# A hybrid encoder block on one core: how the first token block and the warming products start

## The reference

```python
h = rms_norm(x, mix_norm_g[l])
proj = h @ w_in[l]
u_a, v_a, q, k, v = jnp.split(proj, splits, axis=-1)
y_a = spatial_gating(u_a, v_a, sgu_ln_g[l], sgu_ln_b[l], sgu_w[l], sgu_b[l])
y_b = window_sink_attention(...)
x = x + jnp.concatenate([rms(y_a), rms(y_b)], axis=-1) @ w_out[l]
h = rms_norm(x, ffn_norm_g[l])
x = x + (jax.nn.silu(h @ w_gate[l]) * (h @ w_up[l])) @ w_down[l]
return rms_norm(x, final_norm_g)
```

## Time and profile before

| | |
|---|---|
| median of 3 runs | 918.92 us (918.57 to 918.98) |
| the profiled execution | 919.09 us, of which the span of the engines' instructions is 917.3 us |
| PE busy | 909.7 us, 99% of the span |
| PEld, DVE, ACT, POOL busy | 82%, 64%, 47%, 43% |
| chain of work that ended last | PE 98%, issue 1%, all others 0% |
| DMA over the span | 158.56 MB, 173 GB/s |

### The profile page before, as it was taken

How to read it: one execution, slowest core, us unless ns; L and a number is a source line. 1 busy time by engine, 2 the same in 40 slices (tenths; PEclk the granted TensorE clock), 3 DMA queues, 4 the chain that set the end, 5 groups by cost and what they waited for, 6 DMA issues and landing times.

```text
span 917.3 us, 11969 instructions
## 1 busy us (share of the span) xinstructions
PE 909.7 (99%) x4229; PEld 750.0 (82%) x4229; DVE 588.9 (64%) x785; ACT 429.6 (47%) x835; POOL 390.4 (43%) x387
## 2 busy tenths in 40 slices
PE   9999999999999999999999999999999999999997
PEld 7888888787878888888888888888888888888885
DVE  5759879986779787464453653736547676544754
ACT  6747547856556543243333333333334454444451
POOL 1559732331244379557485574855754000000021
PEclk9999999999999999999999999999999999999999
DMA  9797453211242372744727437264366996656543
GB/s 330 235 267 232 115 161 105 80 70 70 92 138 88 97 220 69 232 136 134 228 68 233 138 126 227 76 226 146 121 223 248 372 368 192 201 187 203 185 138 138
DMA packets 151487, 158.56 MB, mean 173 GB/s; under 512 B 27576, under 2 KB 109060, under 8 KB 151428
## 3 DMA queue, kind: packets, MB, share of 16 engines
q1 hardware_dynamic: 150756, 157.40, 53.0%
q10 hardware_dynamic: 672, 0.40, 0.1%
HBM read 117.26 MB, written 40.50 MB: 172 GB/s over the span
## 4 chain that ended last, share of the span: by engine, by line
PE 98%; issue 1%; ACT 0%; POOL 0%; DVE 0%; POOLq 0%; ACTq 0%
PE ps L859 31%; PE ps L861 31%; PE ps L860 31%; PE ps L1031 1%; PE ps L1054 1%; PE ps L1043 1%; PE ps L979 1%; PE ps L1125 1%; PE ps L883 0%; PE ps L892 0%; PE ps L895 0%; PE ps L898 0%; PE ps L1000 0%; PE ps L990 0%; PE ps L1061 0%
## 5 line engine op out<-in xcount | busy, mean ns | idle before, releaser
L2116 DVE TENSOR_TENSOR P_lo<-P_raw,P_hi 128x512 fp32r<-128x512 f32 x132 | 119.5, 921 | 83.2 <-ACT P_hi L1554 78.8
L859 PE MATMUL ps<-T_hi,P_hi 128*128 128x512 f32 x352 | 136.9, 389 | 0.0
L860 PE MATMUL ps<-T_lo,P_hi 128*128 128x512 f32 x352 | 136.9, 389 | 0.0
L861 PE MATMUL ps<-T_hi,P_lo 128*128 128x512 f32 x352 | 136.9, 389 | 0.0
L801 POOL TENSOR_TENSOR wd<-wd 128x256 f32<-128x256 f32 x88 | 80.9, 919 | 93.6 <-DMA wd<-in_w_down 88.4
L859 PE MATMUL ps<-rb_hi,ra_hi 128*128 128x512 f32 x308 | 119.8, 389 | 0.0
L860 PE MATMUL ps<-rb_lo,ra_hi 128*128 128x512 f32 x308 | 119.8, 389 | 0.0
L861 PE MATMUL ps<-rb_hi,ra_lo 128*128 128x512 f32 x308 | 119.8, 389 | 0.0
L1668 ACT ACTIVATE ra_hi<-ra 128x512 fp32r<-128x512 f32 x77 | 48.6, 631 | 98.8 <-DMA rb<-w_down_T 61.0
L649 POOL TENSOR_SCALAR late<-late 128x1 f32<-128x1 f32 x12 | 6.0, 503 | 191.7 <-ACT junk L1736 178.1
L2225 DVE TENSOR_TENSOR ra_lo<-ra,ra_hi 128x512 fp32r<-128x512 f32 x77 | 55.7, 723 | 36.4 <-ACT ra_hi L1668 36.0
(11 more groups left out here) (286 smaller groups left out, 2018.0 us busy)
## 6 DMA issues: line engine op xcount, KB each, us to landing
wd<-in_w_down SPq DMA_DIRECT2D x44, 256.0 KB, 3.3
w_down_T<-wd SPq DMA_DIRECT2D x22, 512.0 KB, 5.0
ra<-act_S SPq DMA_DIRECT2D x44, 256.0 KB, 2.7
rb<-w_down_T SPq DMA_DIRECT2D x44, 256.0 KB, 3.0
act_S<-Q SPq DMA_DIRECT2D x33, 256.0 KB, 3.7
ra<-act_A SPq DMA_DIRECT2D x33, 256.0 KB, 4.4
rb<-in_w_down SPq DMA_DIRECT2D x33, 256.0 KB, 5.0
P_raw<-in_w_gate SPq DMA_DIRECT2D x22, 256.0 KB, 3.7
```

Source lines behind the costliest of these rows:

```text
L859: mm(dst, lhs[0], rhs[0], start=start, stop=False, skip_group_check=onto)
L860: mm(dst, lhs[0], rhs[1], start=False, stop=False, skip_group_check=onto)
L861: return mm(dst, lhs[1], rhs[0], start=False, stop=stop, skip_group_check=onto)
L2116: tt(w_l[p, m][:], src[:], w_h[p, m][:].bitcast(F32), ALU.subtract).then_inc(w_split, 1)
```

## The change

GpSimd first fills a new 128x128 tile `zeros` (in the space of `v_sb0`, which is first written long after), and then does what it did. The warming products now take `zeros` as both operands, in `fp32r` and as plain products, not as transposes; there are 18 of them; and they wait for the first fill alone. TensorE's wait for `ident` stands behind them.

The tokens of block 0 come in two loads of 256 columns: the first counts into a new semaphore `hT0_in`, to which the gains' load moves too; the second into `block_in[0]`. VectorE rounds each half by itself, and TensorE starts with the first half's two tiles. ScalarE's first rounding waits for the weights alone. VectorE also rounds the tokens of block 1 (`hT_hi[0]`, k = 1), which was ScalarE's work. The counts of the waits on `hT_hi_ready` go down by one for that.

```diff
--- before.py
+++ after.py
@@ -67,6 +67,7 @@
     wv_hi, wv_lo = at("wv_hi", 64, [P, K, C], F32R), at("wv_lo", 80, [P, K, C], F32R)
     xs = [at(f"xs{s}", 96 + 4 * s, [P, D]) for s in range(4)]
     v_sb = [at(f"v_sb{s}", 112 + 2 * s, [P, DA]) for s in range(4)]
+    zeros = at("zeros", 112, [P, P], F32R)
     by_offset = at("by_offset", 120, [CH, HB, KW])
     rel_rep = at("rel_rep", 126, [CH, NBUCK, HB])
     w_hi = [at(f"w_hi{s}", 128 + 8 * s, [P, K, P], F32R) for s in range(2)]
@@ -294,7 +295,7 @@
         return IN_PRODUCTS + NP * i + IDX[p, m] + 1
 
 
-    WARM = 15
+    WARM = 18
 
     ROOT_BANK, MIX_BANK = (2, 7), (3, 4)
 
@@ -306,7 +307,8 @@
         def sem(name):
             return ctx.enter_context(nc.semaphore(name))
 
-        ident_set, ident_ready, consts_ready, zero_ready = (sem(n) for n in ("ident_set", "ident_ready", "consts_ready", "zero_ready"))
+        fill_set, ident_ready, consts_ready, zero_ready = (sem(n) for n in ("fill_set", "ident_ready", "consts_ready", "zero_ready"))
+        hT0_in = sem("hT0_in")
         wv0_in, rel_in, setup_in, ffng_in, fin_in = (
             sem(n) for n in ("wv0_in", "rel_in", "setup_in", "ffng_in", "fin_in"))
         bias_out, bias_in, rel_built = sem("bias_out"), sem("bias_in"), sem("rel_built")
@@ -369,9 +371,15 @@
                 sp.dma_start(xs[r % 4][:], xt[r]).then_inc(x_in[r % 4], 16)
 
             def xT_load(h, k):
-                if h:
-                    sp.wait_ge(hT_hi_ready, max(k, 1))
-                sp.dma_start(hT_raw[h][:, k, :], xT[h, k]).then_inc(block_in[k], 16)
+                if h and k < 2:
+                    sp.wait_ge(hT0_hi_ready, k + 2)
+                elif h:
+                    sp.wait_ge(hT_hi_ready, k - 1)
+                if h or k:
+                    sp.dma_start(hT_raw[h][:, k, :], xT[h, k]).then_inc(block_in[k], 16)
+                else:
+                    sp.dma_start(hT_raw[0][:, 0, 0:2 * P], xT[0, 0, :, 0:2 * P]).then_inc(hT0_in, 16)
+                    sp.dma_start(hT_raw[0][:, 0, 2 * P:C], xT[0, 0, :, 2 * P:C]).then_inc(block_in[0], 16)
 
             def item_load(n):
                 sp.dma_start(raw[n][:].rearrange("p (k n) -> p k n", k=K), w_in_k[:, :, COL[ITEMS[n]]:COL[ITEMS[n]] + P]).then_inc(raw_in[n], 16)
@@ -639,9 +647,10 @@
 
         @block.gpsimd
         def _(pool):
-            nc.gpsimd.memset(ident[:], 0.0).then_inc(ident_set, 1)
+            nc.gpsimd.memset(zeros[:].bitcast(F32), 0.0).then_inc(fill_set, 1)
+            nc.gpsimd.memset(ident[:], 0.0).then_inc(fill_set, 1)
             nc.gpsimd.memset(minus_half, -0.5).then_inc(consts_ready, 1)
-            pool.wait_ge(ident_set, 1)
+            pool.wait_ge(fill_set, 2)
             nc.gpsimd.affine_select(out=ident[:], in_=ident[:], compare_op=ALU.not_equal, fill=1.0, base=0,
                                     pattern=[[-1, P]], channel_multiplier=1).then_inc(ident_ready, 1)
 
@@ -878,17 +887,17 @@
                     last = nc.tensor.transpose(ps[:, ROOT_BANK[h], t * P:(t + 1) * P], rstd_x[:, r:r + 1].to_broadcast([P, P]), ident[:])
                 last.then_inc(rstd_T, 1)
 
+            pe.wait_ge(fill_set, 1)
+            for n in range(WARM):
+                mm(ps[:, 0, 0:P], zeros[:], zeros[:], start=True, stop=True)
             pe.wait_ge(ident_ready, 1)
-            for n in range(WARM):
-                nc.tensor.transpose(ps[:, 0, 0:P], ident[:], ident[:])
 
             for k in range(2):
-                if k:
-                    pe.wait_ge(hT_hi_ready, k)
-                else:
-                    pe.wait_ge(hT0_hi_ready, 1)
+                pe.wait_ge(hT0_hi_ready, 3 if k else 1)
                 pe.wait_ge(wv_hi_ready, k + 1)
                 for t in range(HT):
+                    if k == 0 and t == 2:
+                        pe.wait_ge(hT0_hi_ready, 2)
                     mm(ps[:, t, :], hT_hi[0][:, k, t * P:(t + 1) * P], wv_hi[:, k], start=k == 0, stop=False)
                 pe.wait_ge(wv_split, k + 1)
                 for t in range(HT):
@@ -1250,7 +1259,7 @@
 
             def wv_block(k):
                 if k == 0:
-                    act_e.wait_ge(wv0_in, 32)
+                    act_e.wait_ge(wv0_in, 16)
                 else:
                     act_e.wait_ge(block_in[k], LOADED[k])
                 actv(wv_hi[:, k, :], wv_raw[k // 2][:, k % 2, :], ACT.Copy).then_inc(wv_hi_ready, 1)
@@ -1267,10 +1276,12 @@
                 act_e.wait_ge(raw_in[n], 16)
                 actv(w_hi[n][:].rearrange("p k n -> p (k n)"), raw[n][:], ACT.Copy).then_inc(w_hi_ready, 1)
 
-            act_e.dma_start(mix_g, mix_gT).then_inc(wv0_in, 16)
+            act_e.dma_start(mix_g, mix_gT).then_inc(hT0_in, 16)
             for k in range(K):
                 wv_block(k)
-                if k:
+                if k == 1:
+                    act_e.wait_ge(hT0_in, 32)
+                if k > 1:
                     xT_block(0, k)
             for r in range(HT):
                 xT_block(1, 2 * r)
@@ -1761,10 +1772,10 @@
             copy = nc.vector.tensor_copy
 
             def xT_lo(h, k):
-                if h or k:
-                    dve.wait_ge(hT_hi_ready, K * h + k)
-                else:
-                    dve.wait_ge(hT0_hi_ready, 1)
+                if h or k > 1:
+                    dve.wait_ge(hT_hi_ready, K * h + k - 1)
+                else:
+                    dve.wait_ge(hT0_hi_ready, k + 2)
                 stt(hT_lo[h][:, k, :], hT_raw[h][:, k, :], mix_g[:, k:k + 1], hT_hi[h][:, k, :].bitcast(F32), ALU.mult, ALU.subtract).then_inc(hT_ready, 1)
 
             def wv_block(k):
@@ -1819,10 +1830,14 @@
                                   sinks_rep[rows].rearrange("p (g a b) -> p g a b", g=KV, a=2)[:, :, :, t2], -1.0, None, ALU.mult)
                 last.then_inc(sinks_ready, 1)
 
-            dve.wait_ge(wv0_in, 32)
+            dve.wait_ge(hT0_in, 32)
+            ts(hT_hi[0][:, 0, 0:2 * P], hT_raw[0][:, 0, 0:2 * P], mix_g[:, 0:1], None, ALU.mult).then_inc(hT0_hi_ready, 1)
             dve.wait_ge(block_in[0], LOADED[0])
-            ts(hT_hi[0][:, 0, :], hT_raw[0][:, 0, :], mix_g[:, 0:1], None, ALU.mult).then_inc(hT0_hi_ready, 1)
+            ts(hT_hi[0][:, 0, 2 * P:C], hT_raw[0][:, 0, 2 * P:C], mix_g[:, 0:1], None, ALU.mult).then_inc(hT0_hi_ready, 1)
             for k in range(K):
+                if k == 1:
+                    dve.wait_ge(block_in[1], LOADED[1])
+                    ts(hT_hi[0][:, 1, :], hT_raw[0][:, 1, :], mix_g[:, 1:2], None, ALU.mult).then_inc(hT0_hi_ready, 1)
                 wv_block(k)
                 xT_lo(0, k)
             xT_lo(1, 0)
```

## The result

| | before | with the change |
|---|---|---|
| median | 918.58 us (22 runs, 917.68 to 919.15) | 919.94 us (22 runs, 918.59 to 923.09) |
| ratio | | 1.0015, 95% interval 1.0009 to 1.0021 |
| profiled execution | 919.09 us, span 917.3 | 919.11 us, span 917.3 |
| PE busy | 909.7 us | 910.2 us |

The change makes the kernel 1.4 us slower. That is within the 0.2% that was called "same", but the interval excludes no change, and 919.94 lies above the forecast range of 917.1 to 919.0. The two profiled executions differ by 0.02 us (919.09 and 919.11): the one lies near the upper end of the runs of its kernel, the other near the lower end. So a comparison of these two traces shows how each step goes, but not what it costs in the median; the medians of the experiments have to tell that.

A forecast was written before the change was run, and what follows sets the result against it. TensorE, busy 909.7 of 917.3 us, was taken as the bound. Block 2 starting at 10.17 + 0.1 = 10.3 instead of 11.82 took 919.09 to 917.6; the median, 0.17 lower, gave 917.4 us, range 917.1 to 919.0.

The forecast's parts named there:

- TensorE sets the end, and what the start loses goes through: Whole kernel: TensorE sets the end from 1.5 us on, so what its first products gain reaches the end.
- Zeros first; start at 0.97: Start of warming: GpSimd fills zeros from 0.72 to 0.92, so TensorE starts at 0.97, not 1.51.
- 0.213 for each product: Warming on TensorE: each 128x128 zero product takes 0.213 us at the low clock, 18 of them 3.83.
- The clock is up by the first real product: TensorE's start: clock rises at about 4.0, first real product at 4.6, block 2 starts 1.5 us sooner.
- 0.1 + 5.47: From TensorE's first real product to block 2: 0.1 us filling plus 5.47 for 24 products at the high clock.
- The transposes had not raised the clock: Warming before the change: 3.4 us of transposes left the clock low; it rose 2.5 us into real products.
- nearly all there is to win: First eight real products: the low clock costs 3.20 - 1.82 = 1.38 us, nearly the whole possible gain.
- first rival: TensorE's warming: clock rises as before, at about 7.4; time 918.7 to 918.9; chance 0.22.
- second rival: TensorE's clock: rise shifts from run to run, gain anywhere from 0 to 1.5 us, middle 918.1; chance 0.10.
- The data for the first product: Block 0's load: first half of tokens lands at 4.05, rounding costs 0.27, ready at about 4.4.
- One more DMA issue, 0 to 0.25 us: SyncE's loads: the extra issue takes 0.47 us, mostly hidden; block 1 delays TensorE by 0 to 0.25, taken as 0.1.
- VectorE rounds block 1: Block 1's tokens: rounded by 7.03, needed at 7.44; without this part TensorE would have waited 0.4 us.

The follow-up runs named there:

- e6_zeros512: Kernel before with 9 warming products of 512 columns on zeros in place of the 15 transposes: 918.15 us, ratio 0.9998.
- e9_rows: Kernel before with block 0's tokens loaded by two DMAs of 64 rows each: 918.86 us against 918.47, ratio 1.0007.
- e1_warm: Kernel before with 18 products of 128x128 on zeros in place of the 15 transposes, nothing else changed: 919.94 us against 918.48, ratio 1.0013.
- e11_nowarm: Kernel before with its 15 warming transposes taken out, nothing else changed: 920.12 us against 918.63, ratio 1.0014.
- e5_ones128: Kernel before with 18 products of 128x128 on a tile of ones in place of the 15 transposes: 919.31 us, ratio 1.0012.
- e7_ones512: Kernel before with 9 warming products of 512 columns on ones in place of the 15 transposes: 918.24 us, ratio 1.0000.
- e8_best: Kernel before with 8 zero products of 512 columns reading a 128-column tile four times over, VectorE rounding block 1, one token load: 918.17 us against 918.47, ratio 0.9998.
- e3_dve1: Kernel before with VectorE instead of ScalarE rounding block 1's tokens, nothing else changed: 918.61 us, ratio 1.0001.
- e2_split: Kernel before with block 0's tokens in two loads of 256 columns, nothing else changed: 918.91 us against 918.48, ratio 1.0008.
- e10_after512: The whole change with 9 warming products of 512 columns on zeros in place of 18 of 128: 918.84 us against the kernel before, ratio 1.0003.

## Why the prediction was wrong

*TensorE sets the end, and what the start loses goes through.* Right: no later wait took it up or gave it back. In all fourteen traces the time of the profiled execution is the start of block 2 plus 906.9 to 907.4 us, though that start lies anywhere from 10.69 (e6_zeros512, 917.86 us) to 13.06 (e9_rows, 920.03).

*Zeros first; start at 0.97.* Right, 0.98. *0.213 for each product.* Right to the digit.

*The clock is up by the first real product.* This step failed, and with it the sign. The forecast took its price from the right rows and then let the clock rise at about 4.0 with nothing but the kind of the instruction to rest on. With the short zero products the first eight real ones still ran mostly at the low clock, and the median was that without warming (e1_warm 919.94, e11_nowarm 920.12). Ones in the tile made no difference that shows (e5_ones128 919.31). Where the clock was up by the first real product, as in the trace of e6_zeros512, the price was right: block 2 came 10.69 - 4.98 = 5.71 us after the first real product, where 0.1 + 5.47 was forecast.

*The transposes had not raised the clock.* This reading of the trace led there, and it was false. It came from one execution, in which the clock rose late, and that execution, at 919.09, was slower than 21 of the 22 timed ones. The transposes are worth 1.5 us in the median (e11_nowarm). So the change took away a warming that worked. And the 1.38 us that were "nearly all there is to win" were read off that one late rise: products of 512 columns, after which the clock rose within the first four real products or before them, end 0.08 to 0.31 us below before in the median (e6_zeros512, e7_ones512, e8_best), not separated from it. The gain of 1.5 us was not there to be had. The first rival had the mechanism, "short products on zeros load TensorE no better", but priced it against the transposes as if they were worth nothing: 918.8 and not 920. No rival had the loss of what was removed; that is the row missing from the list of what the change removes.

The rule of the Trainium skill that stood beside it (page "TensorE: Matmul & The Clock Gate", Part 4: transposes don't count as work for the clock as matmuls do) does not hold for these float32 transposes of 128x128: with them 918.63, without them 920.12. By that rule the two would have been equal. (The traces list them as MATMUL like the others, so they don't show in which mode TensorE made them.) In the prediction the doubt about that rule is said to give the second rival its large chance; it is the first, with 0.22, to which it belongs.

*The rise comes at another moment of each run* (second rival). True of before as well: 22 runs of one kernel spread over 1.5 us. Four executions that agreed within 0.5 us were too few to argue against it. In the profiled executions of e3_dve1, the kernel before and e9_rows, all with the same 15 transposes, the high spacing begins within the first, the second and the third four real products. Part 1 of the same page of the Trainium skill says that the rise shifts from run to run, and these traces agree.

*The data for the first product.* The first half came at 4.00 where 4.05 was forecast; its rounding took 0.35, not 0.27. Neither mattered.

*One more DMA issue, 0 to 0.25 us.* Too small. The second half came more than a us after the first, block 1 0.94 later than before and block 2 about as much, twice the 0.47 of an issue. The cover named, busy DMA engines with loads queued, was there but in the wrong place. Busy time by stretch in the kernel before (us, PE, PEld, DVE, ACT, POOL, PEclk, DMA share, GB/s):

```profile
3.50:4.50 1.00, 1.00 (x6) 1.00 (x6) 0.12 (x1) 0.63 (x1) 0.00 (x0) 1.00 0.90 272
...
3.00:5.50 2.50, 2.50 (x11) 2.07 (x10) 1.12 (x3) 0.63 (x1) 0.00 (x0) 1.00 0.94 305
```

and with the change:

```profile
3.50:4.50 1.00, 1.00 (x7) 1.00 (x6) 0.35 (x1) 0.63 (x1) 0.00 (x0) 1.00 0.73 116
...
3.00:5.50 2.50, 2.50 (x12) 2.31 (x11) 0.35 (x1) 0.63 (x1) 0.00 (x0) 1.00 0.80 196
...
4.90:7.40 2.50, 2.50 (x6) 1.58 (x6) 1.62 (x3) 0.00 (x0) 0.00 (x0) 1.00 0.96 343
```

From 4.90 to 7.40, the stretch that the forecast read the earlier trace rows, the engines are as busy as before and move as much. What is missing was lost ahead of it: between 3.5 and 4.5 they moved less than half as much and were less busy too, and from 3.0 to 5.5 they moved 2.5 x (305 - 196) = 272 KB less, about the 256 KB of one block's tokens. At the later 343 GB/s that is an estimated 0.8 us, near the 0.94 by which block 1 is late. In the median the split alone is 0.4 us (e2_split), within its uncertainty; in the changed kernel the low clock covered part of it, since TensorE came to block 1 late anyway.

*VectorE rounds block 1.* Costed as hidden unless TensorE came early; e3_dve1 shows no difference by itself, as that implies.

**The sum** in medians: of the change's 1.36 us, 1.0 goes with the length of the warming products (e10_after512); the rest, 0.37, is of the size of what the split shows alone, 0.43. Neither of these two small amounts is separated from nothing. The parts timed alone (1.46, 0.43 and 0.13) come to 2.0, more than the whole, which fits a split whose cost is partly covered while the clock is low; that cover was read from the traces and not timed by itself. The best combination, e8_best, is not shown to be faster than the kernel before.

## What to carry to other kernels

Before replacing something that only prepares, such as warming products, take it out once and time that: its worth can't be seen in a trace of the kernel that has it. Where the moment of an event shifts from run to run, one profile shows one draw; place the profiled execution among the timed ones before reading a cause from it. And a load at the start that is split so that its first half lands 0.4 us sooner can make the blocks queued behind it land about a us later.

## What the runs showed of the hardware that was not expected

- Warming products of 128 columns and of 256 columns in `fp32r`, each with its own weight load, lie equally far apart at the low clock, 0.213 us; the median with the former is not told from that of a kernel without warming (919.94 and 920.12), with the latter not from that of the transposes (918.61 against 918.63).
- Float32 transposes against an identity of the same 128x128, also 0.213 apart, bring the clock up early often enough to be worth 1.5 us in the median, though not in each run: in four traces with them it rose once as late as after eight real products (e9_rows). Why they do and plain 128-column products don't is not settled by these runs.
- Two loads in place of one slowed the DMA as a whole for a stretch between 3.5 and 4.5 us: from 272 GB/s to 116 with rows of 1 KB (112 in e2_split), to 223 with rows of 2 KB (e9_rows). Why is not settled.
